# A hybrid decoder layer: the order of the first loads and sums, and the queue of one small store

## The reference

```python
ada = silu(c) @ w_ada + b_ada
shift1, scale1, gate1, shift2, scale2, gate2 = split(ada, 6)
h = rms_norm(x) * (1 + scale1) + shift1
q_a, k_a, v_a, q_g, k_g, v_g, g_out, z_lr = split(h @ w_in)
attn = sliding_window_attention(q_a, k_a, v_a, sinks, rel_bias)   # 8 heads, window 128
gla  = gated linear attention of q_g, k_g, v_g, gate from z_lr    # 4 heads, chunks of 64
gla  = rms_norm(gla) * gla_norm_g * silu(g_out)
x = x + gate1 * (concat(attn, gla) @ w_out)
h = rms_norm(x) * (1 + scale2) + shift2
x = x + gate2 * (relu(h @ w_mlp_in) ** 2 @ w_mlp_out)
out = rms_norm(x) * final_norm_g
```

## Time and profile before

| | |
|---|---|
| time, median of 3 runs | 1072.1 us (1071.4 to 1073.1) |
| the profiled execution | 1073.1 us, of which the span is 1071.3 |
| TensorE busy | 1029.2 us, 96% |
| VectorE busy | 700.6 us, 65% |
| ScalarE busy | 474.3 us, 44% |
| GpSimd busy | 96.0 us, 9% |
| DMA | 164.74 MB, 154 GB/s in the mean |

### The profile page before, as it was taken

One profiled execution on the slowest core, in us unless ns is written; L12 is line 12 of the kernel. 1 busy time (PEld: TensorE's weight loads), 2 busy tenths in 40 slices (PEclk: granted clock), 3 DMA queues, 4 the chain that ended last, 5 costly groups with the idle time before them and its releaser, 6 DMA issues.

```text
span 1071.3 us, 12935 instructions
## 1 busy us (share of the span) xinstructions
PE 1029.2 (96%) x5003; PEld 823.5 (77%) x5003; DVE 700.6 (65%) x921; ACT 474.3 (44%) x785; POOL 96.0 (9%) x123
## 2 busy tenths in 40 slices
PE   4999999989999999899999999999999999999997
PEld 4577887766666788777888888888888888888885
DVE  3565767697878343798565546645539964478886
ACT  7321012367677112566544554545534243434443
POOL 0101210023223000000000000000141000001100
PEclk9999999999999999999999999999999999999999
DMA  9967831300001703226353444317997422464533
GB/s 335 305 180 251 283 132 40 79 2 1 1 1 41 235 1 126 110 79 216 138 177 140 166 154 167 141 59 266 349 364 271 144 91 106 159 214 158 199 116 157
DMA packets 94019, 164.74 MB, mean 154 GB/s; under 512 B 15475, under 2 KB 44556, under 8 KB 93836
## 3 DMA queue, kind: packets, MB, share of 16 engines
q1 hardware_dynamic: 82076, 121.42, 33.3%
q0 software_dynamic: 11888, 42.55, 11.2%
HBM read 126.19 MB, written 39.33 MB: 155 GB/s over the span
## 4 chain that ended last, share of the span: by engine, by line
PE 85%; DVE 10%; ACT 3%; issue 2%; DMA 1%; SPq 0%; DVEq 0%; ACTq 0%
PE bank L1134 28%; PE bank L1115 25%; PE bank L868 14%; PE bank L680 8%; PE bank L796 2%; PE bank L899 1%; DVE small L1451 1%; DVE prob L1445 1%; PE bank L748 1%; DVE h_lo_T L1601 1%; PE bank L932 1%; ACT gla_out L2032 1%; DVE up_lo L1561 1%; PE bank L756 1%; DVE gla_out L1506 1%
## 5 line engine op out<-in xcount | busy, mean ns | idle before, releaser
L1134 PE MATMUL bank<-dn_hi,hid_hi 128*128 128x512 f32 x448 | 174.3, 389 | 0.0
L1134 PE MATMUL bank<-dn_lo,hid_hi 128*128 128x512 f32 x448 | 174.3, 389 | 0.0
L1134 PE MATMUL bank<-dn_hi,hid_lo 128*128 128x512 f32 x448 | 174.3, 389 | 0.0
L2202 ACT ACTIVATE hid_hi<-hid_raw 128x1024 fp32r<-128x1024 f32 x56 | 58.9, 1051 | 154.0 <-PE bank L1134 154.0
L1690 DVE TENSOR_TENSOR hid_lo<-hid_raw,hid_hi 128x1024 fp32r<-128x1024 f32 x56 | 68.3, 1220 | 84.7 <-ACT hid_hi L2202 84.7
L868 PE MATMUL bank<-w_hi,act_hi 128*128 128x512 f32 x256 | 102.3, 400 | 0.9 <-DVE w_lo L1200 0.9
L1115 PE MATMUL bank<-h_hi_T,up_hi 128*128 128x512 f32 x256 | 100.0, 391 | 1.6 <-DVE h_lo_T L1601 1.5
L1561 DVE TENSOR_TENSOR up_lo<-up_raw,up_hi 128x1024 fp32r<-128x1024 f32 x48 | 58.7, 1223 | 63.5 <-ACT up_hi L2105 63.4
L868 PE MATMUL bank<-w_hi,act_lo 128*128 128x512 f32 x256 | 99.9, 390 | 0.0
L868 PE MATMUL bank<-w_lo,act_hi 128*128 128x512 f32 x256 | 99.7, 390 | 0.0
L1115 PE MATMUL bank<-h_hi_T,up_lo 128*128 128x512 f32 x256 | 99.6, 389 | 0.0
(11 more groups left out here) (247 smaller groups left out, 1927.6 us busy)
## 6 DMA issues: line engine op xcount, KB each, us to landing
hidden_forms<-hid SPq DMA_DIRECT2D x56, 512.0 KB, 3.2
hid_raw<-hidden_forms SPq DMA_DIRECT2D x56, 512.0 KB, 4.0
ada_w<-in_w_ada POOLq DMA_DIRECT2D x32, 512.0 KB, 7.0
up_raw<-in_w_mlp_in SPq DMA_DIRECT2D x32, 512.0 KB, 5.6
dn_ring<-in_w_mlp_out POOLq DMA_DIRECT2D x24, 512.0 KB, 5.9
raw<-in_w_in SPq DMA_DIRECT2D x36, 256.0 KB, 4.8
ada_chunk<-in_w_ada SPq DMA_DIRECT2D x16, 512.0 KB, 9.1
dn_t<-in_w_mlp_out POOLq DMA_DIRECT2D x16, 512.0 KB, 7.6
```

The lines of the kernel that those rows point to most:

```text
L1134: mm = pe.matmul(b, (hid_hi, hid_lo)[x][n % 2][:, k, t * P:(t + 1) * P], (dn_hi, dn_lo)[y][n % 2][:, k, :], start=(first and i == 0), stop ...
L2202: a.activation(hid_hi[n % 2][:, ks, :], hid_raw[n % 2][:, ks, :], ACT.Copy).then_inc(s_dhi, 1)
```

## The change

Three edits, which leave every instruction in place and move some of them.

1. SyncE issues slot 0's weights ahead of chunk 0 of ada. ScalarE and VectorE split their first half earlier, and half 1's turned blocks and chunk 0's sum and columns are put into another order on TensorE, ScalarE and VectorE.
2. On TensorE, the sums of chunks 2 and 3 go between the halves of `first_slot` of one block, `chunk_columns(2)` comes one half block sooner, `z_sum(0)` comes ahead of chunk 3's sum, and `chunk_columns(3)` comes behind `first_slot(4, 1)`.
3. The store of the bias rows is issued by GpSimd, behind the loads of part 2 of ada and ahead of those of part 3, with its wait for `s_rows`. SyncE waits for it to land and issues `bias_copies` ahead of the fill of slot 5.

```diff
@@ -420,8 +420,8 @@
                     sp.dma_start(ident[:, :], identity).then_inc(s_ident, 16)
                 sp.dma_start(x_in[:, t, :], x_d[:, t, :]).then_inc(s_x[t], 16)
             sp.dma_start(b_rows, b_ada[0].rearrange("(k p) -> k p", p=P)).then_inc(s_b_rows, 16)
+            fill(0, 0, columns(w_in_d, QG0))
             ada_first(0)
-            fill(0, 0, columns(w_in_d, QG0))
             ada_first(1)
             sp.wait_ge(s_set, 3)
             with nc.allow_non_contiguous_dma(reason="16 columns of each row"):
@@ -458,14 +458,11 @@
             for s, c0 in ((3, K0), (4, KG0)):
                 fill(s, s % 2, columns(w_in_d, c0))
 
-            sp.wait_ge(s_rows, 1)
-            sp.dma_start(bias_rows.ap(), rows_sb).then_inc(s_rows_out, 16)
+            sp.wait_ge(s_rows_out, 16)
             one_row = bass.AP(tensor=bias_rows, offset=0, ap=[[0, P], [1, HEADS * 384]])
+            sp.dma_start(bias_copies.ap(), one_row).then_inc(s_bias, 16)
             for s in range(4):
                 fill(SLOT_T + s, (SLOT_T + s) % 2, wide_rows((VG0, GO0)[s // 2], s % 2))
-                if s == 0:
-                    sp.wait_ge(s_rows_out, 16)
-                    sp.dma_start(bias_copies.ap(), one_row).then_inc(s_bias, 16)
             sp.wait_ge(s_bias, 16)
             sp.wait_ge(s_gate_s, 8)
             sp.wait_ge(s_gate_v, 8)
@@ -593,6 +590,9 @@
                         pool.wait_ge(s_ada_used, j - 3)
                     pool.dma_start(ada_w[:, j % 4, :], w_ada_d[:, k, part * D:(part + 1) * D])\
                         .then_inc(s_ada_w[j % 4], 16)
+                if part == 2:
+                    pool.wait_ge(s_rows, 1)
+                    pool.dma_start(bias_rows.ap(), rows_sb).then_inc(s_rows_out, 16)
             pool.wait_ge(s_ada_used, 4 * KT)
             pool.memset(w_gate[:, :], 0.0).then_inc(s_set, 1)
             pool.wait_ge(s_set, 5)
@@ -804,10 +804,11 @@
             pe.transpose(bank[5][:, 0:6 * KT], b_rows, ident[0:6 * KT, 0:6 * KT]).then_inc(s_b_full, 1)
             pe.wait_ge(s_set, 4)
             chunk_sum(0, 0)
+            turn_half(1, range(4))
             chunk_sum(0, 1)
-            turn_half(1, range(4))
+            turn_half(1, range(4, 6))
             chunk_columns(0)
-            turn_half(1, range(4, KT))
+            turn_half(1, range(6, KT))
             chunk_sum(1, 0)
             first_slot(0, 0)
             chunk_sum(1, 1)
@@ -815,19 +816,19 @@
             chunk_columns(1)
             first_slot(1, 0)
             first_slot(1, 1)
+            chunk_sum(2, 0)
             first_slot(2, 0)
-            chunk_sum(2, 0)
             chunk_sum(2, 1)
             first_slot(2, 1)
+            chunk_columns(2)
             first_slot(3, 0)
-            chunk_columns(2)
             first_slot(3, 1)
+            z_sum(0)
             chunk_sum(3, 0)
+            first_slot(4, 0)
             chunk_sum(3, 1)
-            z_sum(0)
+            first_slot(4, 1)
             chunk_columns(3)
-            first_slot(4, 0)
-            first_slot(4, 1)
             for half in range(2):
                 first_slot(5, half)
             for half in range(2):
@@ -1317,13 +1318,13 @@
             v.tensor_scalar(b_col[:, KT:2 * KT], b_col[:, KT:2 * KT], 1.0, None, ALU.add).then_inc(s_b_col, 1)
             turned_out(1, 0)
             turned_out(1, 2)
+            first_half_lo()
             v.wait_ge(s_b_col, 1)
             first_columns(0)
             norm_affine(0)
             turned_out(1, 4)
-            first_half_lo()
+            turned_out(1, 6)
             norm_lo(0)
-            turned_out(1, 6)
             norm_affine(1)
             norm_lo(1)
             second_half_lo()
@@ -1953,12 +1954,12 @@
                 .then_inc(s_nrm[1], 1)
             for k in range(3, KT):
                 turned_out(0, k)
-            chunk_sum_out(0)
+            first_half_hi()
             turned_out(1, 1)
             turned_out(1, 3)
-            first_half_hi()
+            chunk_sum_out(0)
+            turned_out(1, 5)
             norm_hi(0)
-            turned_out(1, 5)
             turned_out(1, 7)
             norm_hi(1)
             second_half_hi()
```

## The result

| | before | changed |
|---|---|---|
| median | 1072.6 us (1071.4 to 1074.0, 4 runs) | 1081.7 us (1080.3 to 1082.9, 4 runs) |
| the profiled execution | 1073.1, span 1071.3 | 1080.5, span 1078.7 |

The changed kernel is slower by a ratio of 1.0084 (95% interval 1.0066 to 1.0102), 9.1 us between the medians. The forecast was slower by 5.5 us, 1077.6, within 1072.0 to 1080.0: the direction came, the size didn't, and the range ended too low.

What follows compares the result with a forecast made beforehand. TensorE, busy 96% of the span, was taken as the bound. A 3.8 us delay at part 3, including 0.4 from edits 1 and 2, plus 1.7 of slow clock gave 5.5: 1077.6 us against the median, range 1072.0 to 1080.0.

Steps and rivals of the forecast that it cites:

- -0.1: Edit 1, TensorE's first wait: first_slot(0, 0) starts 0.1 us sooner, waiting 1.9 us instead of 2.0, slow clock unchanged.
- +0.4: Edits 1 and 2 together, early part up to slot 0's last matmuls: 0.4 us slower net, bounds +0.1 to +0.9.
- -0.15: Edit 2, before first_slot(2, 0): chunk_sum(2, 0) fills the short wait there, a gain of 0.15 us.
- +0.3 and +0.6: Edit 2, late chunk_columns(3): TensorE waits 0.3 us before first_slot(6, 0) and 0.6 us before first_slot(7, 0).
- 0.1 to 0.2: Edit 2, the two pairs between chunk 3's columns and first_slot(6, 0): 0.1 to 0.2 us allowed for starts.
- the bounds of 115.2 and 117.6: Edit 3, VectorE's end of part 3: lower value 115.2 us, upper bound 117.6, delayed by late loads beside the copies.
- The 3.8: Edit 3, columns of part 3: TensorE restarts at 116.3 instead of 112.49, 3.8 us, the early 0.4 inside it.
- The 1.7: Slow clock behind the new TensorE wait: priced at 1.7 us, the same as behind the first wait of 2.0.
- A: Rival, part 3's loads come in time and TensorE doesn't wait at 112: 1072.5 us, chance 0.18.
- B: Rival, the slow clock behind the first wait goes, 1.7 us back, loads in time too: down to 1070.1, chance 0.08.
- C: Rival, VectorE misses part 3 by under 2 us and no slow clock follows: 1074 us, chance 0.14.
- D: Rival, queues pass everything first, and part 4 is late or the slow clock longer: 1080 to 1081 us, chance 0.1.

Runs made afterwards that it cites:

- e3: The kernel before with edit 1 alone: 1071.9 us, ratio 0.9998.
- e4: The kernel before with edit 2 alone: 1073.5 us, ratio 1.0012.
- e12: The kernel before with only chunk 3's columns moved behind both halves of block 4: 1072.9 us, ratio 1.0013.
- e6: The changed kernel with GpSimd's wait and store moved behind the first four loads of part 3: 1073.5 us, ratio 1.0009.
- e9: The changed kernel with the copies of the bias rows issued behind slot 6's fill: 1073.3 us, ratio 1.0009.
- e2: The kernel before with edit 3 alone: 1082.1 us, ratio 1.0091.
- e10: The kernel before with only GpSimd's wait for the bias rows added behind part 2's loads: 1080.1 us, ratio 1.0070.
- e1: The changed kernel with edit 3 undone, so edits 1 and 2 only: 1073.2 us, ratio 1.0010.
- e13: The kernel before with 6 extra float32 matmuls in TensorE's first wait: 1071.8 us, ratio 0.9996.
- e14: The kernel before with edit 1, chunk 2's two sums together ahead of block 2, and 5 extra matmuls in the first wait: 1071.9 us, ratio 0.9997.
- e5: The changed kernel with 18 extra matmuls nobody reads ahead of the columns of part 3: 1078.7 us, ratio 1.0059.
- e11: The changed kernel with 26 extra matmuls nobody reads ahead of the columns of part 3: 1078.1 us, ratio 1.0060.

## Why the prediction was wrong

**Edit 1: right.** Forecast -0.1; e3 gives no difference, and the first wait is 1.7 us instead of 1.9. One detail was off: TensorE came to chunk 0's first half at 20.2 instead of 21.0, just as it landed, and waited 0.16 us for it. The last `raw` load of slot 0 was issued between 16.0 and 16.3, as the earlier trace rows say, not between 15.7 and 16.0; nothing hangs on it.

**Edit 2: right in kind, too small.** I had +0.4 with edit 1, and e4 gives +1.3. My own terms make more than I wrote: -0.1, -0.15, +0.3 and +0.6 add up to +0.65. The late columns cost 0.95 (e12), about the 0.9 that I had. The other moves were to gain 0.15, and they cost 0.35 net. If the 0.15 was gained, alternating sums and products cost 0.5 us (an estimate), and I had allowed 0.1 to 0.2 for it.

**Edit 3: the mechanism was right.** VectorE was to end part 3 at 116.2, between the bounds of 115.2 and 117.6, and it did at 116.24. That it lies between them is the sum's merit; that it agrees to the tenth is luck. I had picked 116.2 between the bounds, the loads began 1 us sooner than I had them, and the DMA engines moved more, and faster, than I had:

```profile
DMA packets 2056, 7.40 MB, mean 341 GB/s; under 512 B 247, under 2 KB 255, under 8 KB 1927
```

That is from 93.2 to 114.92, where load 15 lands; I had 6.8 MB at 305 GB/s. The loss needs what I named, the lost prefetch and the copies on the same DMA engines: e6 brings the prefetch back and e9 takes the copies away, and either alone ends the wait.

**The step that failed is the price of that end on TensorE, 3.8 + 1.7 = 5.5.** Both terms were too small, for different reasons:

- The 3.8. I measured the delay from 112.49, where the columns of part 3 start in the profile of before. That execution had the slow clock behind its first wait, which cost it 1.5 us and which no other profile had. In e3, without it, the same columns start at 110.89. Since the end of part 3's loads hardly depends on when TensorE arrives, the true delay is counted from there: 116.3 - 110.9 = 5.4 us. Edit 2 brings TensorE's arrival to 111.8 and leaves a wait of 4.5.
- The 1.7. I priced the slow clock by the stretch behind a wait of 2.0 us, though the new wait was to be nearly twice as long. Behind 4.5 to 5.1 us the clock was low for 6.8 to 9.4 us of work, which cost 3.3 to 4.7 (3.4 in the changed kernel).

5.4 + 3.4 = 8.8 us, against 9.1 measured between the medians.

**The rivals.** A did not come: VectorE was 4 us late. Nor did B: the slow clock behind the first wait is gone in the changed kernel's profile, but the typical execution of before doesn't have it, so nothing comes back in the median. C did not come. D, with 0.1, was nearest in time (1080 to 1081), by a longer slow clock, which it named; part 4 did not miss, and VectorE did not end later than forecast. The range ended at 1080.0 because I cut D's upper part off; with it, it would have gone to 1081, still under the 1081.7 measured. The chances for a time within 0.2% add up to 0.33, not to 0.31.

**The sentences on the Trainium skill.** The figure of the Trainium skill for a DMA of GpSimd's queue ("DMA: Bandwidth & Descriptors", Anatomy of one DMA) gives an estimate of 3.2 us for 512 KB. It does not hold beside other traffic: part 3's eight loads took 4.1 to 11.8 us in the changed kernel, and the last six of them 7.0 or more. With the copies away (e9), the median of nine loads was 5.8 us, beside slot 5's weights, and VectorE's eight steps followed each other at 1.3 to 2.4 us. In the two microseconds of the earlier trace rows the two queues sent 48 and 46 packets, about as many each, though 0.59 MB against 0.19.

What stays open: why the slow clock behind 4.5 us lasts twice as long as that behind 2.0 us, and why it lasted 9.4 us in e2 and 6.8 in e10.

## What to carry to other kernels

A wait put into a queue of prefetches delays every load behind it to the wait's end, however cheap the transfer that it guards; ask which loads were issued before that time, and what else the DMA engines do when they come instead. When loads come late, price their end against where the consumer arrives in a typical execution, not in the profiled one: look whether a slow stretch of the clock ahead of it is there in every profile. And with the slow clock behind it, a wait of 4.5 to 5.1 us on TensorE cost 1.7 to 1.9 times its length here; filling it with matmuls that nobody reads gave back 3 us, moving the wait behind four loads gave back 8.

## What the runs showed of the hardware

- Behind one and the same wait the slow clock comes in some executions and not in others. Behind the first wait, 1.7 to 2.0 us, it came in one profile of thirteen. Every profile also has two later waits that no edit touches: 1.8 us before L997, about 223 us into the span (231 in the changed kernel), and about 2.5 us before L1115, at 490 to 500 us (line numbers of the kernel before). A slow clock followed the first of these in ten of the seventeen profiles and the second in seven. In e3 and e4 it followed both, as here in e4; in e1 and e6 neither, and the clock fell only behind TensorE's last matmul.

```profile
222.00:228.00 6.00, 4.63 (x27) 3.27 (x28) 4.42 (x11) 1.77 (x3) 3.63 (x2) 0.72 0.00 0
490.00:497.00 7.00, 4.95 (x15) 3.94 (x16) 4.46 (x6) 5.40 (x8) 0.00 (x0) 0.76 0.98 289
```

- This is a large part of the spread between executions of one kernel. From slot 1's first product to the span's end it takes 1004.2 us in e1 and e6, 1005.0 in before and e12 (slow behind the first of the two waits), 1005.7 in e13 and e14 (behind the second), and 1006.8 and 1007.4 in e3 and e4. What decides it is not shown.
- In the profile of e5 TensorE was idle for only 0.5 us, followed by 16 matmuls one column wide, and the clock fell 1.5 us behind the start of these; in that of e11 the same columns without the idle time left it at 1.00.
- From 93.2 to 107.5 us the DMA engines moved 4.92 MB in e9 without the copies and 4.72 MB in the changed kernel with them, but GpSimd's share of it was 3.86 MB against 2.70.
